# Ten projection tiles as five pairs of two by two block products, seven products for eight, joined on VectorE

## The chip, the cores and the metric

The kernel runs on one core of a Trainium2 chip. The time is device microseconds (us) of one execution. Before the change three executions took 1659.24, 1662.63 and 1664.48 us, median 1662.63. TensorE (PE) multiplies and writes PSUM, VectorE (DVE) does elementwise work, ScalarE (ACT) does activations and copies, GpSimd (POOL) does elementwise work on SBUF only and starts some of the DMAs, SyncE (SP) starts the others.

## The reference

One decoder layer with four parallel token mixers, then a mixture of experts, for 1024 prompt tokens and 8 sample tokens (1032 in all). Everything is float32. The part that matters here is the first projection and what the RWKV mixer does with its first seven tiles:

```python
proj = h @ lw['w_in']                     # h: 1032 x 1024; first 21 tiles of 128 columns feed the mixers
prev = jnp.concatenate([shift0[:, None, :], p[:, :-1]], axis=1)
q = p + (prev - p) * lw['rwkv_mu']        # "interpolation" with the token before, on 7 of the tiles
```

The other tiles feed a pooling branch (2 tiles), a convolution branch (4) and a state-space branch (8). 32 more tiles of the same projection are gates. What is computed stays the same in the changed kernel up to rounding, since a seven-product scheme adds and subtracts blocks before and after the products.

## The kernel before

The normalised input lies in SBUF as `H`, 128 partitions by 8 slices (`k`) by 1032 tokens. A projection tile is a 1024 by 128 piece of the weights (512 KB), stored as eight 128 by 128 blocks in one of the two halves of the ring `wring`. For each tile PE runs three chunks of 344 tokens. A chunk is eight matmuls, one for each `k`, accumulated in one PSUM bank (`half`, L499). A float32 matmul appears in the trace as two weight loads and two matmul records, so a chunk is 16 records and a tile 48.

Tiles 0 to 2 have code of their own (L514, L520, L534), since the norm is still being computed. Tiles 3 to 12 are `pairs(1, 3)` and `pairs(3, 6)`. Tile 13 is cut into pieces that stand between the small products of the RWKV branch (L551, L562). Then come `pairs(7, 10)`, the first gate tiles, and a loop of eight steps in which gate tiles fill PE between small dependent products. The last sections are the branch outputs (L812), the output projection (L861) and the experts (L961, L975).

ACT copies each finished chunk from PSUM into its slot of `PR` (`evac`, L1029) and counts the semaphore `evac`. PE waits for `evac` before it writes a bank again. SP loads the next tile into the ring half that has come free, after a count of `dense` (finished chunks).

In the stretch of tiles 3 to 12 DVE does one thing: when seven RWKV tiles are in SBUF (`evac` 21) it interpolates them, three instructions for each (L1373 to L1375). When two pooling tiles are there (`evac` 27), POOL runs the windowed sums of the pooling branch (L1900 to L1927), about fifty instructions in a row.

The order on each engine is written out by hand. Nothing is scheduled.

Of the kernel before, what the change touches and what calls it, by code (L numbers as in the profile page):

```python
# [57 lines left out]
ROUND = 1.5 * 2 ** 23  # L58
GUESS = [0, 4, 8, 13]
# [80 lines left out]
def build(nc, ins, outs):  # L140
    ctx = ExitStack()
    with ctx:
# [88 lines left out]

        x_t = carve(0, KT, T)
# [42 lines left out]

        block = ctx.enter_context(nc.Block())
# [29 lines left out]
        def mm_of(t, k):  # L306
            return 7 * t + k + (2 if t or k > 1 else 0)

        def ev_of(t, k):
            return 2 + 11 * t + k  # L310

        def sum_of(t, k):
            return k if t == 0 else 4 * t + 4 + k
# [46 lines left out]
        def _(sp):  # L360
# [15 lines left out]
            for j in range(1, N_BR0 // 2 + 1):  # L376
# [106 lines left out]
        def _(pe):  # L483
# [53 lines left out]
            pairs(1, 3)  # L537
            pairs(3, 6)


# [5 lines left out]
            for t in range(2):  # L546
                pe.wait_ge(sem("lora_act"), t + 3)
                if t == 1:
                    pe.wait_ge(sem("k_ss"), 1)
                for c in range(NCH):  # L550
                    mm = pe.matmul(ps[:, 3 + c, 0:CW], bones, TM[:, t, chunk(c)], start=True, stop=True)  # L551
                mm.then_inc(sem("head_sum"), 1)
                tile13(1, 2 * t, 2 * t + 2)
# [263 lines left out]
            def turn(p):  # L817
                m, b = rows_of(ORD[p]), 4 + 2 * (p % 2)
                pe.wait_ge(sem("h2_row"), p + 1)
                if p == 0:  # L820
                    pe.wait_ge(sem("out_c"), 2)
# [46 lines left out]
            for t in range(4):  # L868
# [5 lines left out]
                if t == 0:  # L874
                    for h in range(2):
                        pe.wait_ge(sem("out_c"), h + 1)
# [6 lines left out]
                pe.wait_ge(sem("out_ev"), ev_of(t - 1, 11) if t else 1)  # L883
                pe.wait_ge(sem("op_sum"), sum_of(t, 3))
                if t == 0:
                    pe.wait_ge(sem("op_sum"), 4 + 2)
# [3 lines left out]
                pe.wait_ge(sem("out_c"), 2 + t + 1)  # L890
# [9 lines left out]
                if t == 0:  # L900
                    pe.wait_ge(sem("op_sum"), 4 + 3)
# [3 lines left out]
                if t == 0:  # L905
                    pe.wait_ge(sem("op_sum"), 4 + 4)
# [99 lines left out]
        def _(act):  # L1006
# [37 lines left out]
            for t in range(2):  # L1044
                A(TM[:, t, :], row(S_K + t), ACT.Square, scale=v("kkw", t)).then_inc(sem("lora_act"), 1)
# [192 lines left out]
            def norm_row(p):  # L1238

                n, m = ORD[p], rows_of(ORD[p])  # L1240
                act.wait_ge(sem("out_ev"), ev_of((p - 1) // 2, 7 if p % 2 else 11) if p else 2)
# [77 lines left out]
        def _(dve):  # L1319
# [44 lines left out]


            dve.wait_ge(sem("evac"), 21)
            dve.wait_ge(sem("pads"), 1)
            dve.wait_ge(sem("h_ready"), KT + 1)
            nc.vector.tensor_copy(shift_out[:, :, :], PR[:, S_R:S_R + 7, PAD + TP - 1:]).then_inc(sem("lerp"), 1)
            dve.wait_ge(sem("lerp"), 1)  # L1370
            for t in range(7):
                s = S_R + t
                tt(TM[:, t % 2, 0:TP], PR[:, s, PAD - 1:PAD + TP - 1], row(s, 0, TP), SUB)  # L1373
                link(tt(TM[:, t % 2, TP:T], shift_in[:, t, :], row(s, TP, T), SUB))
                stt(row(s), TM[:, t % 2, :], v("mu", t), row(s), MUL, ADD).then_inc(sem("lerp"), 1)  # L1375
# [315 lines left out]
            def weight_sum(j, left, right):  # L1691

                if j:
                    dve.wait_ge(sem("op_sum"), 4 + j)
# [9 lines left out]
            for h in range(2):  # L1704
                r_ = X2[0:NSMP, NTT - 1, h * HALF:(h + 1) * HALF]
                dve.wait_ge(sem("out_mm"), h + 2)
# [10 lines left out]
            for t in range(4):  # L1717
                bank = [ps[:, (7 * t + k) % 3, :] for k in range(7)]
                (r11, r12), (r21, r22) = ([X2[:, 2 * t + s, h * HALF:(h + 1) * HALF] for h in range(2)] for s in range(2))
                dve.wait_ge(sem("out_c"), 2 + t + 1)  # L1720
# [487 lines left out]
```

## Time and profile before

| | |
|---|---|
| median of three executions | 1662.63 us |
| profiled execution, its own time | 1668.07 us |
| span of the profiled execution | 1666.3 us |
| PE busy | 1549.1 us (93%) |
| DVE busy | 690.7 us (41%) |
| ACT busy | 351.8 us (21%) |
| POOL busy | 200.8 us (12%) |
| mean granted TensorE clock | 0.970 of 2.4 GHz |

PE is the engine to look at. Over 84% of the span the chain that ended last runs through it. Line L499, which holds the projection tiles and gate tiles, has 37% of the span alone. Busy times count what the engine does, not whether the end waits for it. Idle time of DVE, ACT or POOL costs nothing unless PE stands and waits for them.

### The profile page before, as it was taken

What the parts mean: (1) busy time and instruction counts of PE and PEld (TensorE: products, weight loads), DVE (VectorE), ACT (ScalarE), POOL (GpSimd) and SP (SyncE); (2) the same over time, 40 slices, a digit from 0 to 9 for tenths busy, and PEclk for the clock granted to TensorE, in tenths of its full rate; (3) what the DMA queues carried; (4) which work ended last, traced back from release to release, by engine and by line L of the source; (5) the groups of instructions that cost most, each with busy time, mean ns of one, the idle gap of its engine ahead of it and who ended that gap; (6) DMA issues with size and microseconds to landing.
All of it is one profiled execution on the core that took longest, in us unless ns stands there. A gap on an engine that the chain in (4) does not pass through costs nothing.

```text
span 1666.3 us, 20478 instructions
## 1 busy us (share of the span) xinstructions
PE 1549.1 (93%) x7925; PEld 971.2 (58%) x7925; DVE 690.7 (41%) x1300; ACT 351.8 (21%) x653; POOL 200.8 (12%) x316
## 2 busy tenths in 40 slices
PE   8999999999999999999999999999999298888965
PEld 5666666577777777777777865666444232222312
DVE  5130069943343535436353433577844401101106
ACT  3000230231313131313313135000122111111113
POOL 3006300012111111111010010100000001101100
PEclk9999999999999999999999999999999599989987
DMA  6111111021421322121113121474200958766547
GB/s 197 38 39 39 35 37 39 27 111 53 114 64 53 115 52 63 44 72 47 44 39 122 52 92 42 152 289 174 112 38 30 370 196 334 260 226 236 204 153 294
DMA packets 47377, 195.73 MB, mean 117 GB/s; under 512 B 6424, under 2 KB 6920, under 8 KB 42416
## 3 DMA queue, kind: packets, MB, share of 16 engines
q1 hardware_dynamic: 28288, 117.18, 20.3%
q0 software_dynamic: 18992, 77.25, 12.9%
q8 instruction: 63, 1.03, 0.3%
q14 instruction: 34, 0.28, 0.1%
HBM read 357.43 MB, written 41.44 MB: 239 GB/s over the span
## 4 chain that ended last, share of the span: by engine, by line
PE 84%; DMA 5%; DVE 4%; issue 2%; SPq 2%; ACT 2%; POOL 0%; DVEq 0%; POOLq 0%; ACTq 0%
PE ps L499 37%; PE ps L812 7%; PE ps L961 6%; PE ps L861 6%; PE ps L975 4%; PE ps L756 3%; DMA arena<-in_w_gu 3%; PE ps L670 2%; PE ps L665 2%; PE ps L675 2%; PE ps L648 2%; SPq L428 1%; PE ps L514 1%; PE ps L940 1%; PE ps L520 1%
## 5 line engine op out<-in xcount | busy, mean ns | idle before, releaser
L499 PE MATMUL ps<-arena,wring 128*128 128x344 f32 x2208 | 667.2, 452 | 0.0
L499 PEld LDWEIGHTS ps<-arena,wring 128*128 128x128 f32 x2208 | 405.1, 189 | 191.0 <-issue 1.9
L961 PE MATMUL ps<-arena,scr 128*32 128x512 f32 x1280 | 151.8, 620 | 20.3 <-DMA arena<-in_w_gu 20.3
L1955 POOL DMA_DIRECT2D gate_scratch<-stage x96 | 52.3, 545 | 619.7 <-ACT stage L1101 544.1
L812 PE MATMUL ps<-arena,wring 128*128 128x344 f32 x384 | 111.2, 451 | 0.0
L961 PEld LDWEIGHTS ps<-arena,scr 128*32 128x32 f32 x1280 | 39.0, 112 | 116.1 <-issue 82.6
L812 PEld LDWEIGHTS ps<-arena,wring 128*128 128x128 f32 x384 | 72.5, 189 | 38.6
L975 PE MATMUL ps<-arena,scr 128*32 128x512 f32 x640 | 79.6, 642 | 13.7 <-issue 12.3
L1101 ACT ACTIVATE stage<-ps 128x344 f32<-128x344 f32 x84 | 38.4, 458 | 253.6 <-PE ps L499 253.5
L1843 DVE TENSOR_TENSOR scr<-scr,ps 128x256 f32<-128x256 f32 x20 | 8.4, 421 | 187.1 <-ACT scr L1284 187.1
L1540 DVE TENSOR_TENSOR scr<-scr,ps 128x512 f32<-128x512 f32 x40 | 27.5, 688 | 127.8 <-PE ps L670 127.8
L1414 DVE SCALAR_TENSOR_TENSOR arena<-arena,vec 128x1024 f32<-128x1024 f32 x60 | 74.4, 1283 | 1.1
L1029 ACT ACTIVATE arena<-ps 128x344 f32<-128x344 f32 x57 | 25.9, 458 | 225.1 <-PE ps L499 208.0
L975 PEld LDWEIGHTS ps<-arena,scr 128*32 128x32 f32 x640 | 22.9, 118 | 69.6 <-issue 68.0
L756 PE MATMUL ps<-arena,wring 128*128 128x344 f32 x192 | 59.1, 469 | 3.3 <-ACT stage L1075 3.3
L861 PE MATMUL ps<-arena,scr 128*128 128x512 f32 x128 | 58.2, 599 | 0.0
L756 PEld LDWEIGHTS ps<-arena,wring 128*128 128x128 f32 x192 | 37.6, 197 | 24.5 <-ACT stage L1075 3.9
L1141 ACT ACTIVATE scr<-ps 128x512 f32<-128x512 f32 x40 | 23.9, 597 | 130.4 <-PE ps L665 130.4
L2072 POOL DMA_INDIRECT y_rows<-scr,idx x20 | 19.6, 982 | 246.4 <-DVE scr L1856 241.7
L665 PEld LDWEIGHTS ps<-scr 128*128 128x128 f32 x320 | 41.9, 191 | 8.0
L670 PEld LDWEIGHTS ps<-scr 128*128 128x128 f32 x320 | 41.9, 191 | 8.0
L1856 DVE COPY scr<-ps 128x512 f32<-128x512 f32 x20 | 13.8, 692 | 74.0 <-PE ps L975 74.0
(430 smaller groups left out, 1883.7 us busy)
## 6 DMA issues: line engine op xcount, KB each, us to landing
arena<-in_w_gu SPq DMA_DIRECT2D x336, 512.0 KB
arena<-in_w_dn SPq DMA_DIRECT2D x84, 1024.0 KB
wring<-in_w_all SPq DMA_DIRECT2D x61, 512.0 KB, 3.6
gate_scratch<-stage POOLq DMA_DIRECT2D x96, 172.0 KB, 2.2
arena<-gate_scratch POOLq DMA_DIRECT2D x4, 2064.0 KB, 9.5
scr<-gate_scratch POOLq DMA_DIRECT2D x4, 2064.0 KB, 9.5
arena<-y_rows SPq DMA_DIRECT2D x16, 512.0 KB, 10.8
arena<-in_w_out SPq DMA_DIRECT2D x2, 2048.0 KB, 14.9
```

Of the source, the lines that this page charges most:

```text
L499: mm = pe.matmul(ps[:, c, 0:CW], wring[:, slot, k, :], H[:, k, chunk(c)], start=k == 0, stop=k == KT - 1)
L648: mm = pe.matmul(ps[:, 4 + n, (q % 2) * 256:(q % 2) * 256 + 256], (BT if n < 2 else KTB)[:, q, :], KR[:, q, :, :].rearrange("p a b -> p (a ...
L665: mm = pe.matmul(ps[:, 6, q * P:(q + 1) * P], NLB[:, q, :], U[:, q, :], start=True, stop=True)
L670: mm = pe.matmul(ps[:, 7, q * P:(q + 1) * P], TT[:, q, :], X1[:, q, :], start=True, stop=True)
L756: mm = pe.matmul(ps[:, 6 + m % 2, 0:CW], wring[:, n % 2, k, :], H[:, k, chunk(c)], start=k == 0, stop=k == KT - 1)
L812: mm = pe.matmul(ps[:, m % 6, 0:CW], wring[:, n % 2, 2 * b + k, :], row(2 * b + k, c * CW, (c + 1) * CW), start=k == 0, stop=k == 1)
L861: mm = pe.matmul(ps[:, bank, :], left[:, k, :], right[:, k, :], start=k == 0, stop=k == 3)
L961: mm = pe.matmul(ps[S * j:S * (j + 1), i % 2, :], XT[i % 2][:, k * P + S * j:k * P + S * (j + 1)], GU[j][:, k * 2 * HID:(k + 1) * 2 * HID] ...
L975: mm = pe.matmul(ps[S * j:S * (j + 1), 5 + h, :], ATB[:, k, S * j:S * (j + 1)], DN[j][:, k * D + h * HALF:k * D + (h + 1) * HALF], start=k ...
L1101: A(stage[:, c, :], ps[:, c, 0:CW], ACT.Sigmoid).then_inc(sem("evac"), 1)
L1414: ins_ = ts(dst, src, w, v("conv_b", t), MUL, ADD) if j == 0 else stt(dst, src, w, dst, MUL, ADD)
L1955: pool.dma_start(gate_scratch[:, g:g + 1, chunk(c)], stage[:, c:c + 1, :]).then_inc(sem(f"gate_out{c}"), 16)
```

## The change

PE now makes tiles 3 to 12 in five pairs (`pair_tiles`, L620 of the changed kernel). A pair is a product of 1024 by 256 weights with 1024 by 1032 tokens. It is cut into two halves along all three sides: 512 rows, 128 columns (one tile), 516 tokens. Seven block products take the place of eight. Each is done in two quarters of 258 tokens, four matmuls each. The seven results rotate through six PSUM banks.

DVE makes the sums and differences of the weight blocks (`pair_sums`, four for each pair), once those of the tokens (`weight_sum_in`, four in all), and it joins the products (`pair_add`, 14 for each pair). ACT only copies the first product of each pair to SBUF. The seven interpolations (`lerp`) no longer stand in a row. They stand between the joins of the pairs 2 and 3. The weights of a pair lie in two places at once, so a second pair of buffers is used in turn with the ring. The interpolation and two ScalarE squares use other scratch (`TML` in place of `TM`).

```diff
+        PAIRW = [[kk_ring(0), kk_ring(1)], [wring[:, 1, :, :], wring[:, 0, :, :]]]
+        BS = [carve(4 * HT2 * j, 4, HT2) for j in range(4)]          # HT2 = 516, QT = 258
...
 SP:
+            load_pair(0, (0,))
+            sp.wait_ge(sem("dense"), 3)
+            load(2, 0)
+            load_pair(0, (1,))
+            sp.wait_ge(sem("dense"), 9)
+            load_pair(1)
+            for t in range(2, NPAIR):
+                sp.wait_ge(sem("dense"), 6 * t + 3)
+                load_pair(t)
...
 PE:
-            pairs(1, 3)
-            pairs(3, 6)
+            def pair_tiles(t):
+                wa, wb = PAIRW[t % 2]
+                left = (wa[:, 0:4, :], wa[:, 4:8, :], AS[1], AS[0], AS[3], AS[2], wb[:, 4:8, :])
+                right = ((H[:, 0:4, :], 0), (H[:, 4:8, :], 0), (BS[1], None), (BS[0], None), (H[:, 4:8, :], 1), (BS[2], None), (BS[3], None))
+                sums = (0, 0, 3, 1, 4, 2, 0)
+                weight_sums = (0, 0, 2, 1, 0, 3, 4)
+                last_read = (None, 1, 3, 5, 7, 10, 13)
...
+                for k in range(7):
+                    for q in range(2):
+                        g = 14 * t + 2 * k + q
+                        if g < 6:
+                            pe.wait_ge(sem("evac"), min(9, 7 + g))
+                        else:
+                            t0, k0, q0 = (g - 6) // 14, (g - 6) % 14 // 2, g % 2
...
+                        if sums[k] and q == 0:
+                            pe.wait_ge(sem("op_sum"), psum(t, sums[k]))
...
+                        for j in range(4):
+                            mm = pe.matmul(ps[:, g % 6, 0:QT], left[k][:, j, :], src[:, j, c], start=j == 0, stop=j == 3)
...
 ACT:
-            for j in range(1, 3):
-                evac(2 * j + S_R + 1, 6 * j + 3)
-                evac(2 * j + S_R + 2, 6 * j + 6)
-            for j in range(3, 6):
-                evac(2 * j - 6, 6 * j + 3)
-                evac(2 * j - 5, 6 * j + 6)
+            for t in range(NPAIR):
+                for q in range(2):
+                    act.wait_ge(sem("out_mm"), pmm(t, 0, q))
...
+                    A(PQ[q], ps[:, (14 * t + q) % 6, 0:QT], ACT.Copy).then_inc(sem("out_c"), 1)
...
 DVE:
+            def pair_sums(t):
...
+                tt(AS[0], wb[:, 0:4, :], wb[:, 4:8, :], ADD).then_inc(sem("op_sum"), 1)
+                tt(AS[2], wa[:, 0:4, :], wb[:, 0:4, :], SUB).then_inc(sem("op_sum"), 1)
...
+            def pair_add(t, k, dst, left, q, after=None):
...
+                ins_ = tt(dst, left, ps[:, (14 * t + 2 * k + q) % 6, 0:QT], ADD)
+                if q and k in (4, 6):
+                    ins_.then_inc(sem("evac"), 3)
...
+                for q in range(2):
+                    pair_add(t, 5, row(nb)[:, cols(1, q)], VQ[q], q)
+                    pair_add(t, 5, row(nb)[:, cols(0, q)], UQ[q], q)
+                if t < NPAIR - 1:
+                    pair_sums(t + 1)
+                for q in range(2):
+                    pair_add(t, 6, row(nb)[:, cols(0, q)], row(nb)[:, cols(0, q)], q, pev(t, 10 + 2 * q))
...
+            pair_sums(0)
+            weight_sum_in(0, H[:, 0:4, HT2:T], H[:, 0:4, 0:HT2])
...
+            pair_joins(0)
+            pair_joins(1)
...
+            pair_joins(2, (0, 1, 2, 3))
+            pair_joins(3, (4, 5, 6))
+            pair_joins(4)
```

On PE, at the start of tile 3, this stood before. Two chunks are shown; `w_in1` is the load of the tile, `evac` the copy out of the bank.

```order
L499 MATMUL ps<-arena,wring 128x344 [waits w_in1,evac]
L499 MATMUL ps<-arena,wring 128x344 x7
L499 MATMUL ps<-arena,wring 128x344 [waits evac]
L499 MATMUL ps<-arena,wring 128x344 x7
L499 MATMUL ps<-arena,wring 128x344 [waits evac]
```

In the changed kernel PE has this where pair 4 starts. The end of pair 3 stands first, then the products 0, 1 and 2 of pair 4. `out_ev` and `evac` are counts of DVE's joins, and `op_sum` counts its block sums.

```order
L620 MATMUL ps<-scr,wring 128x258 [waits out_ev]
L620 MATMUL ps<-scr,wring 128x258 x3
L620 MATMUL ps<-arena 128x258 [waits out_ev,w_in0,w_in1]
L620 MATMUL ps<-arena 128x258 x3
L620 MATMUL ps<-arena 128x258 [waits evac]
L620 MATMUL ps<-arena 128x258 x3
L620 MATMUL ps<-arena 128x258 [waits out_ev]
L620 MATMUL ps<-arena 128x258 x3
L620 MATMUL ps<-scr,arena 128x258 [waits op_sum,out_ev]
```

A chunk of eight matmuls of 344 tokens has become one of four matmuls of 258, and the waits are now for DVE where they were for ACT.

On DVE the seven interpolations stood in a row before, with nothing around them that PE waits for. The start of that row:

```order
L1369 COPY shift_out<-arena 128x63 [waits h_ready,pads,evac]
L1373 TENSOR_TENSOR scr<-arena 128x1024 [waits lerp]
L1374 TENSOR_TENSOR scr<-shift_in,arena 128x8
L1375 SCALAR_TENSOR_TENSOR arena<-scr,vec,arena 128x1032 [waits dve_self]
L1373 TENSOR_TENSOR scr<-arena 128x1024
```

In the changed kernel this is what DVE does in pair 3, from the last of its three interpolations on. L1475 is a join, L1484 to L1486 an interpolation, L1460 to L1465 the sums for pair 4.

```order
L1475 TENSOR_TENSOR arena<-arena,ps 128x258 [waits out_ev,out_mm] x2
L1484 TENSOR_TENSOR arena<-arena 128x1024
L1485 TENSOR_TENSOR arena<-shift_in,arena 128x8
L1486 SCALAR_TENSOR_TENSOR arena<-arena,vec 128x1032 [waits dve_self]
L1475 TENSOR_TENSOR arena<-arena,ps 128x258 [waits out_ev,out_mm] x2
L1475 TENSOR_TENSOR arena<-arena,ps 128x258 [waits out_mm] x4
L1460 TENSOR_TENSOR arena<-arena 128x512 [waits w_in0,w_in1,out_mm]
L1461 TENSOR_TENSOR arena<-arena 128x512
L1463 TENSOR_TENSOR arena<-arena 128x512 [waits op_sum]
L1465 TENSOR_TENSOR arena<-arena 128x512 [waits op_sum]
L1475 TENSOR_TENSOR arena<-arena,ps 128x258 [waits out_ev,out_mm]
L1475 TENSOR_TENSOR arena<-arena,ps 128x258 [waits out_ev,dense]
```

The interpolations moved in among joins whose results free PE's banks, and the sums for pair 4 stand behind all of them.

## Rows read from the trace of the kernel before

**Rows 1.** Busy time of PE, PEld, DVE, ACT, POOL by stretch; then clock, DMA share, GB/s.

```profile
53.20:192.10 138.90, 138.90 (x482) 90.65 (x481) 17.85 (x22) 13.75 (x31) 44.18 (x62) 1.00 0.14 40
192.10:215.80 23.70, 22.69 (x73) 12.48 (x71) 2.46 (x2) 11.20 (x11) 0.00 (x0) 1.00 0.08 22
```

**Rows 2.** Chain of waits from 50 us on: start us, us, what.

```profile
53.23 138.83 PE ps L499 x480
```

**Rows 3.** Chain of waits in the stretch of the branch outputs.

```profile
1062.75 111.05 PE ps L812 x384
```

**Rows 4.** Timeline of PE around one 256-token group: start us, us, engine, line.

```profile
439.05 3.62 PE L648 MATMUL ps<-scr 128*128 128x256 f32 x16
442.51 3.92 PE L499 MATMUL ps<-arena,wring 128*128 128x344 f32 x13
```

**Rows 5.** Timeline of the weight loads of a 128-token group.

```profile
363.57 1.15 PEld L665 LDWEIGHTS ps<-scr 128*128 128x128 f32 x8
```

**Rows 6.** Groups of DVE by form: count | busy us, mean ns | idle before.

```profile
L1684 DVE TENSOR_TENSOR scr<-arena 128x512 f32<-128x512 f32 x4 | 2.8, 689 | 0.0
L1695 DVE TENSOR_TENSOR arena<-arena 128x2048 f32<-128x2048 f32 x4 | 9.1, 2285 | 0.1
L1843 DVE TENSOR_TENSOR scr<-scr,ps 128x256 f32<-128x256 f32 x20 | 8.4, 421 | 187.1 <-ACT scr L1284 187.1
L1373 DVE TENSOR_TENSOR scr<-arena 128x1024 f32<-128x1024 f32 x7 | 8.5, 1218 | 0.0
L1375 DVE SCALAR_TENSOR_TENSOR arena<-scr,vec,arena 128x1032 f32<-128x1032 f32 x7 | 9.1, 1294 | 0.2
```

**Rows 7.** Groups of POOL by form, the three costliest of the pooling sums.

```profile
L1918 POOL TENSOR_SCALAR scr<-scr,cst 64x1008 f32<-64x1008 f32 x4 | 11.2, 2806 | 0.4
L1920 POOL TENSOR_TENSOR arena<-scr,arena 64x1024 f32<-64x1024 f32 x4 | 8.7, 2171 | 0.3
L1906 POOL TENSOR_TENSOR scr<-arena 128x1040 f32<-128x1040 f32 x2 | 3.8, 1921 | 0.2
```

**Rows 8.** Timeline of POOL and DVE where both work on SBUF.

```profile
462.81 2.96 POOL L1964 COPY scr<-arena 64x256 f32<-64x256 f32 x6
463.26 0.69 DVE L1543 TENSOR_TENSOR scr<-scr,ps 128x512 f32<-128x512 f32 x1
463.86 0.77 DVE L1544 TENSOR_TENSOR scr<-scr,cst 128x512 f32<-128x512 f32 x1
```

**Rows 9.** Single lines, ns min/median/max: 374 to 382 us (first two), whole span.

```profile
L1964 POOL COPY scr<-arena x6: 396/399/762, 375.9 to 378.5; 64x256 f32<-64x256 f32 x6
L1550 DVE SCALAR_TENSOR_TENSOR scr<-arena,vec,scr x6: 339/410/517, 377.6 to 379.5; 128x128 f32<-128x128 f32 x6
L1544 DVE TENSOR_TENSOR scr<-scr,cst x32: 682/685/776, 369.7 to 939.0; 128x512 f32<-128x512 f32 x32
```

**Rows 10.** Chain of waits where PE waits for a DVE result.

```profile
199.11 0.03 issue
199.14 0.02 DVEq L1379
199.16 0.05 issue
199.21 1.24 DVE scr L1380
200.45 0.14 issue
```

**Rows 11.** Group of the first small product behind the projection tiles.

```profile
L551 PE MATMUL ps<-scr,cst 128*128 128x344 f32 x12 | 4.0, 467 | 0.7 <-ACT scr L1045 0.4 <-DVE scr L1380 0.3
```

**Rows 12.** Timeline of DVE, before tile 3 and behind its convolution chain.

```profile
47.04 0.16 DVE L1363 TENSOR_SCALAR smallv<-vec 128x2 f32<-128x2 f32 x1
...
323.65 1.23 DVE L1428 TENSOR_TENSOR arena<-ps,arena 128x1032 f32<-128x1032 f32 x1 [0.18 <-PE ps L597]
```

**Rows 13.** Loads of projection tiles, from issue to landing.

```profile
DMA to landing us min/median/max: 3.4/3.6/15.6
```

More of the change, by code:

```diff
@@ L58 @@
 ROUND = 1.5 * 2 ** 23
+NPAIR = 5
+HT2 = T // 2
+QT = T // 4
 GUESS = [0, 4, 8, 13]
@@ L274, in build, with cols, pmm, pev @@
         V1, V2, V3, V4, V5 = (carve(2 * j * T, 2, T) for j in range(5))
+        PAIRW = [[kk_ring(0), kk_ring(1)], [wring[:, 1, :, :], wring[:, 0, :, :]]]
+        BS = [carve(4 * HT2 * j, 4, HT2) for j in range(4)]
+        AS = [arena[:, HO + KT * T + 2 * TP + 512 * j:HO + KT * T + 2 * TP + 512 * (j + 1)].rearrange("p (k m) -> p k m", k=4)
+              for j in range(4)]
+        PQ = [row(11, QT * q, QT * q + QT) for q in range(2)]
+        UQ = [row(10, QT * q, QT * q + QT) for q in range(2)]
+        VQ = [row(10, QT * q + 2 * QT, QT * q + 3 * QT) for q in range(2)]
+        TML = PR[:, 12:14, PAD:]
+        def cols(side, q):
+            return slice(side * HT2 + q * QT, side * HT2 + (q + 1) * QT)
+        def pmm(t, k, q):
+            return 13 * t + 2 * k + q + 1
+        def pev(t, i):
+            return 12 * t + i - (1 if i > 8 else 0)
+        def psum(t, i):
+            return i if t == 0 else 4 + 4 * t + i
         block = ctx.enter_context(nc.Block())
@@ L375, in _, with load_pair @@
             load(1, 1)
-            for j in range(1, N_BR0 // 2 + 1):
+            def load_pair(t, tiles=(0, 1)):
+                for s in tiles:
+                    n = 3 + 2 * t + s
+                    sp.wait_ge(sem(f"w_in{n % 2}"), 16 * (n // 2))
+                    sp.dma_start(PAIRW[t % 2][s].rearrange("p k m -> p (k m)").unsqueeze(1), ins["w_all"][:, bass.ds(n, 1), :]
+                                 ).then_inc(sem(f"w_in{n % 2}"), 16)
+            load_pair(0, (0,))
[7 more added lines that the diff above has]
+                load_pair(t)
+            sp.wait_ge(sem("dense"), 33)
+            sp.wait_ge(sem("w_in1"), 16 * 6)
+            load(13, 1)
+            sp.wait_ge(sem("w_in0"), 16 * 7)
+            load(14, 0)
+            sp.wait_ge(sem("dense"), 42)
+            load(15, 1)
+            for j in range(8, N_BR0 // 2 + 1):
                 sp.wait_ge(sem("dense"), 6 * j - 3)
@@ L1044, in _ @@
             for t in range(2):
-                A(TM[:, t, :], row(S_K + t), ACT.Square, scale=v("kkw", t)).then_inc(sem("lora_act"), 1)
+                A(TML[:, t, :], row(S_K + t), ACT.Square, scale=v("kkw", t)).then_inc(sem("lora_act"), 1)
             for t in range(2):
@@ new lines, in pair_add @@
+            def pair_add(t, k, dst, left, q, after=None):
+                if (k, q) == (6, 1):
+                    dve.wait_ge(sem("dense"), 6 * t + 15)
+                else:
+                    dve.wait_ge(sem("out_mm"), pmm(t, k, q))
+                if after:
+                    dve.wait_ge(sem("out_ev"), after)
+                ins_ = tt(dst, left, ps[:, (14 * t + 2 * k + q) % 6, 0:QT], ADD)
+                if q and k in (4, 6):
+                    ins_.then_inc(sem("evac"), 3)
+                else:
+                    ins_.then_inc(sem("out_ev"), 1)
```

101 lines of the change are left out of this document (80 added, 21 removed).

## Prediction

> **What bounds the kernel now.** I read four views in this order. First the busy times by stretch: from 53.2 to 192.1 us, where tiles 3 to 12 are made, PE is busy for 138.90 of 138.90 us at the full granted clock, while DVE has 17.85 us of work and ACT 13.75 [rows 1]. The stretch is PE's alone. Second the chain of waits: it runs through these tiles as one piece of 138.83 us with 480 records and no gap [rows 2]. So each us that PE saves here is a us off the end, as long as nothing else becomes late. Third the groups of DVE and POOL by form, for the prices of what is added [rows 6, 7]. Fourth the timeline where DVE and POOL work on SBUF together, since the change puts DVE work beside POOL's pooling sums [rows 8, 9].
>
> **PE's part.** A record of 344 tokens costs 138.83 / 480 = 289.2 ns. At two cycles for a token, 344 tokens are 286.7 ns at 2.4 GHz, which leaves 2.5 ns fixed. A record of 258 tokens then costs 215.0 + 2.5 = 217.5 ns. The nearest group of the trace has 256 tokens: from its start to the start of the next group 3.46 us pass for 16 records, or 216.3 ns [rows 4], so 218 ns for 258. The changed kernel has 5 pairs x 7 products x 2 quarters x 4 matmuls = 280 matmuls, 560 records. That is 121.8 us at 217.5 ns and 122.1 at 218. I take **17.0 us saved**; the ends are 16.7 and, had the fixed part been nothing, 18.4.
>
> Do shorter records expose the weight loads? A load takes 0.19 us, and 0.217 is still more. Loads can also follow faster than their own length: eight of them end within 1.15 us where the matmuls have 128 tokens, so (1.15 - 0.19) / 7 = 0.137 us apart [rows 5]. I count nothing. Do more waits cost? In the branch outputs every four records stand behind a wait, and 384 records take 111.05 us, again 289.2 ns each [rows 3]. A wait that is already met costs PE nothing.
>
> **Loads.** SP issues the same ten tiles, now in pairs, one pair ahead. A load lands 3.6 us after its issue, at worst 15.6 [rows 13]; a pair of tiles has the 24.4 us of the pair in front. Two loads one after the other, since each waits for the one before in its half, are 7 us. Nothing.
>
> **DVE's and ACT's part without POOL.** Queued operations start about 0.09 us before the one in front seems to end (463.26 to 463.86 for a 0.69 us operation [rows 8]), so I take a join of 258 tokens from PSUM at 0.34 us (421 ns for 256 [rows 6]), a weight sum of 512 at 0.60, an interpolation (1218 + about 160 + 1294 ns) at 2.55 and a token sum of 2064 at 2.2 [rows 6]. Pair 0: DVE is free at 47.2 us [rows 12], four weight sums and four token sums are 11.2 us, done by 58.5. PE starts the pair at 53.2, needs token sum 1 (the second) at 60.2 and the last at 74. Hidden. A product (two quarters) takes PE 3.48 us. Two joins and one interpolation are 3.23, so DVE keeps up, barely. At the end of a pair: four joins (1.4), four weight sums (2.4), two joins (0.7), and PE asks for the third sum and the first of these joins two products into the next pair. In pair 3, which starts at 53.2 + 3 x 24.36 = 126.3, DVE is through with these by 150.8, and PE asks at 157.7. That is 6.9 us to spare, and between 133.7 and 150.8 DVE has 14.0 us of work in 17.1, so 3 us of idle time can also be eaten. **DVE may lose 10 us in pair 3 before PE stands.**
>
> ACT copies ten quarters where it copied thirty chunks, less than before.
>
> **The end of the stretch.** Tile 13 used to find its bank free. Its first chunk now waits for `evac` 37, which comes only with the very last join of pair 4. From PE to DVE 0.10 us, the join 0.42, from DVE back to PE 0.14 [rows 10, 6]: **0.7 us lost**. Against this, ACT finishes its squares long before PE wants them, since the interpolations end in pair 3 and ACT is free after the two copies at the start of pair 4. The idle time of 0.4 us in front of the first small product [rows 11] goes: **0.4 gained**. Behind it everything starts from the end of tile 13. The long convolution chain on DVE, which is done only 0.2 us ahead of PE at 323.65 [rows 12], starts from it too, so both shift together. The gate tiles, the output products and the experts' weight loads are all triggered by PE's progress. I see nothing tied to absolute time.
>
> **POOL's part, the cost I can bound only.** POOL's pooling sums start at `evac` 27. That was the copy of tile 8, 53.2 + 6 x 13.9 + 0.5 = 137 us; now it is the last join of pair 2, at 127.4. POOL has 44.2 us of work [rows 1], much of it in operations of 1.9 to 2.8 us that stand back to back (ten of them average (11.2 + 8.7 + 3.8) / 10 = 2.37 us [rows 7]). Before, DVE was idle then. Now pair 3 has three interpolations and four weight sums in this stretch, 13 DVE operations with both inputs in SBUF. The trace shows what such neighbours do. Beside six POOL copies of 0.40 us, a DVE operation with one input in PSUM keeps its 0.69 us (L1543), while the one with both in SBUF goes from 685 ns to 0.77 us (L1544), and of six small ones, 339 ns at the least, the median is 410 and the longest 517 ns; one copy goes from 399 to 762 ns, about until the DVE operation ended [rows 8, 9]. So they take turns, and a DVE operation waits for some part of POOL's: 0.17 of 0.40 us in the small ones.
>
> The page "SBUF — State Buffer" of the Trainium skill (Who interferes with whom) says the same against this change: a VectorE instruction with two SBUF inputs contends with a GpSimd instruction that reads SBUF, and one that has the port keeps it for the whole instruction. The trace agrees in who is slowed: L1544 is and L1543 is not. By that rule each of the 13 could wait for a whole POOL operation.
>
> Let w be the mean wait of the 13. PE's stall is 13 w - 10, and not below 0. Bounds: w = 0 gives no stall; a whole large operation, 2.3 us, gives 20 us. The same part as in the small ones, 0.17 / 0.40 of 2.37, is w = 1.0 and 3 us; half an operation, as for one that arrives at any time, is 1.15 and 5 us. The joins have a PSUM input and do not wait. I take the first, **3 us lost**, near the start of pair 4. Pair 4 has no interpolation and no sums, so it ends there. The granted clock is 1.00 in both stretches of [rows 1], the second with 1.0 us of standing in it; that a stall of 3 us would lower it is not in the sum.
>
> **The sum.** -17.0 + 0.7 - 0.4 + 3.0 = -13.7 us. Against the profiled execution's own time, 1668.07 us, that is 1654.4. This execution lies 5.4 us above the median of the three, so for the median: 1662.63 - 13.7 = **1648.9 us**. Executions of before lie 5.2 us apart, so about 0.3% either way is what a measurement cannot tell from no change.
>
> **Rivals.**
>
> *DVE never makes PE stand.* POOL gives way, or its waits stay under 10 us. For it: the slack is large. Against it: the 0.77 us and the 517 ns. Gain 17.0 - 0.3 = 16.7, time 1645.9.
>
> *DVE and POOL alternate operation for operation.* Each of the 13 waits for a whole large POOL operation. For it: half and more of the six small DVE operations were slowed. Against it: POOL also has dozens of 0.2 us operations, the first of a row waits half an operation only, and the 8-token parts of the interpolations hide in the gaps. Stall 13 x 2.3 - 10 = 20, net 17.0 - 0.3 - 20 = -3.3, time 1666; with the 2.8 us operations (26.4) 1672. It costs more than the products save from w = 2.05 on. This is the case on the slow side.
>
> *The pitch does not follow the tokens.* If 258-token records with a new weight block each took 250 ns instead of 217.5 (operands changing between two regions, sums just written), 560 records would be 140 us and the gain gone: 1663. For it: nothing of 258 tokens is in the trace. Against it: the 216.3 ns beside 256 tokens.
>
> *Half is given back later.* The shift lets some transfer or DVE chain behind 320 us become the last to arrive. 1655. For it: DVE's 0.2 us of slack at 323.65. Against it: its chain starts at the same trigger as PE's.
>
> **How the numbers follow.** The forecast (stall of 1 to 7 us) 0.54; no stall 0.22; alternation in full 0.08; pitch 0.05; half given back 0.11. "Faster by over 0.3%" (5 us) takes the first, the second and nearly all of the last: 0.86. "Within 0.3%": part of the pitch and of the alternation, and a bit of the last: 0.09. "Slower": 0.05. The range goes from the no-stall case less a us and a half of spread, 1644, to 1658, which takes in the given-back case and a stall of up to 12 us.
>
> **What would show it.** 560 records on L620 at 217 to 218 ns of pitch; PE's idle time in front of L620 near the product 2 of pair 4, put down to DVE's sums, of about 3 us and nothing at pairs 1 to 3; L1484 and L1486 at 1.22 and 1.29 us in pair 2, and longer in pair 3; the last weight sum for pair 4 at about 160 us; tile 13 starting 0.3 us behind the last product, and all that follows earlier by one amount, up to the end. The prediction is wrong if PE stands at each pair, if the pitch is above 225 ns, or if the shift at the start of the output products is not the one at tile 13.

## The result and the profile after

| | before | after |
|---|---|---|
| median of the executions | 1662.1 us (1659.24 to 1664.48) | 1644.06 us (1640.15 to 1647.82) |
| profiled execution, its own time | 1668.07 us | 1640.67 us |
| PE busy | 1549.1 us | 1523.1 us |
| DVE busy | 690.7 us | 741.2 us |
| mean granted TensorE clock | 0.970 | 0.974 |

After to before is 0.9894, 95% interval 0.9874 to 0.9915: faster by 17.6 us (14.1 to 20.9). Forecast were 13.7 us and 1648.9, from 1644 to 1658. The time lies inside by 0.06 us, at the fast edge. Of the runs below, three executions (4185, 4186 and 1865 us) were disturbed and are left out of every median and range.

The chain of waits (start us, us, what) around the pairs:

```profile
52.35 121.81 PE ps L620 x560
174.16 0.03 DVEq L1474
174.20 0.04 issue
174.24 0.43 DVE arena L1475
174.68 0.04 issue
174.72 4.90 PE ps L552 x16
179.62 1.75 PE ps L639 x6
```

560 records follow each other at 121.81 / 560 = 217.5 ns with no gap. In this place stood 138.83 us [rows 2]. Then comes the stop ahead of tile 13, from 174.16 to 174.72. The first small product (L639) starts straight behind the first chunk of tile 13.

Busy time of PE, PEld, DVE, ACT, POOL by stretch, with clock, DMA share and GB/s, which answers to [rows 1]:

```profile
52.35:174.16 121.81, 121.80 (x560) 105.91 (x559) 62.71 (x110) 9.81 (x16) 44.12 (x48) 1.00 0.13 44
174.16:191.30 17.14, 15.99 (x52) 9.37 (x52) 2.89 (x3) 3.14 (x3) 5.24 (x15) 1.00 0.10 11
```

DVE's work in the stretch has gone from 17.85 to 62.71 us, half of the stretch, and PE never waits for it. The joins, as a group, and the two large parts of the interpolations, as single lines (ns min/median/max):

```profile
L1475 DVE TENSOR_TENSOR arena<-arena,ps 128x258 f32<-128x258 f32 x70 | 27.8, 420 | 58.6 <-PE ps L620 58.2
```

```profile
L1484 DVE TENSOR_TENSOR arena<-arena x7: 1210/1219/1376, 108.5 to 141.5; 128x1024 f32<-128x1024 f32 x7
L1486 DVE SCALAR_TENSOR_TENSOR arena<-arena,vec x7: 1292/1294/3458, 109.8 to 142.9; 128x1032 f32<-128x1032 f32 x7
```

DVE stood idle for 58.2 us ahead of joins because PE had not finished. The reverse did not happen. Of the 14 large parts of interpolations one was held up for long, 3458 ns. The timeline of DVE and POOL shows by what:

```profile
130.83 2.81 POOL L2084 TENSOR_SCALAR scr<-scr,cst 64x1008 f32<-64x1008 f32 x1
132.50 0.42 DVE L1475 TENSOR_TENSOR arena<-arena,ps 128x258 f32<-128x258 f32 x1 [1.32 <-PE ps L620]
132.84 1.22 DVE L1484 TENSOR_TENSOR arena<-arena 128x1024 f32<-128x1024 f32 x1
...
134.18 3.46 DVE L1486 SCALAR_TENSOR_TENSOR arena<-arena,vec 128x1032 f32<-128x1032 f32 x1
134.20 2.35 POOL L2086 TENSOR_TENSOR arena<-scr,arena 64x1024 f32<-64x1024 f32 x1
...
148.35 0.69 DVE L1463 TENSOR_TENSOR arena<-arena 128x512 f32<-128x512 f32 x1
149.08 0.69 DVE L1465 TENSOR_TENSOR arena<-arena 128x512 f32<-128x512 f32 x1
...
149.91 1.92 POOL L2072 TENSOR_TENSOR scr<-arena 128x1040 f32<-128x1040 f32 x1
```

L1486 ended 1.09 us behind POOL's TENSOR_TENSOR, so it had waited for nearly all of it. L1484 beside POOL's TENSOR_SCALAR kept its 1.22 us. The weight sums fell among POOL's operations of 8 tokens and kept 0.69. So the 13 operations in pair 3 waited 3458 - 1294 + 1376 - 1219 ns and little else, 2.3 us: w was 0.18 us, not 1.0. The last weight sum for pair 4 ended at 149.8 us, where the prediction had about 160. POOL's next row of four large TENSOR_TENSORs began at 149.91, 0.14 us behind it.

How the shift travels is read from the chain of waits, us from one mark to the next. The marks are the start of tile 3, the first of the branch gates (L756 before, L844 after), the start of the output products, and the first reload of `y_rows`. The last column is the granted clock of the 272 to 282 us ahead of that reload.

| execution | to branch gates | to output | to y_rows | clock |
|---|---|---|---|---|
| before, three executions | 933.39, 933.31, 933.18 | 197.43, 194.71, 194.72 | 440.1, 436.0, 438.9 | 0.94, 0.95, 0.94 |
| after, three executions | 916.38, 916.63, 916.29 | 194.72, 197.54, 194.71 | 434.3, 432.3, 435.0 | 0.96, 0.97, 0.96 |

Up to the branch gates the change gives 933.29 - 916.43 = 16.9 us, and executions agree within 0.3. The middle has two values in both kernels, 2.8 us apart. They come from one group of 16 records behind a stop of 3.34 us, in which PE waits for ScalarE's copies to `stage`. L844 x16 takes 4.89 us in the profiled execution of after and 7.73 in `e_again`, the same program. The granted clock was 1.00 behind the stop in the first and 0.50 in the second. So the same stop may cost 2.8 us of clock or nothing, and the two kernels have to be compared at the same middle value. (`e_adds`, below, lies between the two.) The rest of the medians' gain lies in the last column but one.

### The profile page after: what moved, and what is told of

Its sections match the earlier page's. It is cut to its first block, busy times and chain, and to the rows that moved or that the text cites. A ratio compares the mean times of both kernels' runs of the same rounds, so it can differ in the third digit from the quotient of the medians.

```text
span 1638.9 us, 20757 instructions
## 1 busy us (share of the span) xinstructions
PE 1523.1 (93%) x8005; PEld 985.3 (60%) x8005; DVE 741.2 (45%) x1394; ACT 342.1 (21%) x633; POOL 205.7 (13%) x316
## 4 chain that ended last, share of the span: by engine, by line
PE 84%; DMA 6%; DVE 4%; issue 2%; SPq 2%; ACT 2%; POOL 0%; DVEq 0%; POOLq 0%; ACTq 0%
PE ps L552 29%; PE ps L620 7%; PE ps L900 7%; PE ps L949 6%; PE ps L1049 5%; PE ps L1063 4%; PE ps L844 3%; DMA arena<-in_w_gu 3%; PE ps L758 2%; PE ps L753 2%; PE ps L763 2%; PE ps L736 2%; SPq L481 1%; DMA scr<-h_rows,idx 1%; PE ps L567 1%
## 5 line engine op out<-in xcount | busy, mean ns | idle before, releaser
L552 PE MATMUL ps<-arena,wring 128*128 128x344 f32 x1728 | 528.5, 452 | 0.6 <-DVE arena L1475 0.6
L552 PEld LDWEIGHTS ps<-arena,wring 128*128 128x128 f32 x1728 | 314.4, 189 | 143.5 <-issue 1.9
L1049 PE MATMUL ps<-arena,scr 128*32 128x512 f32 x1280 | 146.7, 605 | 17.0 <-DMA arena<-in_w_gu 17.0
L900 PE MATMUL ps<-arena,wring 128*128 128x344 f32 x384 | 111.2, 451 | 0.0
L900 PEld LDWEIGHTS ps<-arena,wring 128*128 128x128 f32 x384 | 72.5, 189 | 38.6
L1063 PE MATMUL ps<-arena,scr 128*32 128x512 f32 x640 | 78.2, 632 | 16.1 <-issue 14.8
L620 PE MATMUL ps<-scr,arena 128*128 128x258 f32 x288 | 64.3, 381 | 0.0
L844 PE MATMUL ps<-arena,wring 128*128 128x344 f32 x192 | 56.4, 453 | 3.3 <-ACT stage L1163 3.3
L620 PEld LDWEIGHTS ps<-scr,arena 128*128 128x128 f32 x288 | 54.6, 190 | 8.0
L949 PE MATMUL ps<-arena,scr 128*128 128x512 f32 x128 | 58.2, 598 | 0.0
L1475 DVE TENSOR_TENSOR arena<-arena,ps 128x258 f32<-128x258 f32 x70 | 27.8, 420 | 58.6 <-PE ps L620 58.2
L844 PEld LDWEIGHTS ps<-arena,wring 128*128 128x128 f32 x192 | 36.1, 189 | 23.3 <-ACT stage L1163 3.9
```

Of the source, the lines that this page charges most:

```text
L552: mm = pe.matmul(ps[:, c, 0:CW], wring[:, slot, k, :], H[:, k, chunk(c)], start=k == 0, stop=k == KT - 1)
L620: mm = pe.matmul(ps[:, g % 6, 0:QT], left[k][:, j, :], src[:, j, c], start=j == 0, stop=j == 3)
L844: mm = pe.matmul(ps[:, 6 + m % 2, 0:CW], wring[:, n % 2, k, :], H[:, k, chunk(c)], start=k == 0, stop=k == KT - 1)
L900: mm = pe.matmul(ps[:, m % 6, 0:CW], wring[:, n % 2, 2 * b + k, :], row(2 * b + k, c * CW, (c + 1) * CW), start=k == 0, stop=k == 1)
L949: mm = pe.matmul(ps[:, bank, :], left[:, k, :], right[:, k, :], start=k == 0, stop=k == 3)
L1049: mm = pe.matmul(ps[S * j:S * (j + 1), i % 2, :], XT[i % 2][:, k * P + S * j:k * P + S * (j + 1)], GU[j][:, k * 2 * HID:(k + 1) * 2 * HID] ...
```

## The experiments

**The change alone, again.** Unchanged kernels, for the spread: `e_again` and `e_third` are the changed one, `b_again` and `b_third` the one before.

> The changed kernel itself once more, timed in five rounds. Theory: the gain is the 17.0 us of the records (560 at 217.5 ns for 480 at 289.2), less 0.66 us in front of tile 13, plus 0.4 us at the first small product, and nothing else. So the stretch from the first record of tile 3 to the first record after tile 13's first chunk is 16.7 us shorter, and the median of five rounds lies 16 to 18 us below before. Rival: something behind 320 us gained too (the profiled execution was 27 us shorter than the one of before). Then the median is 19 us or more below before, and the start of the output products is again 20 us earlier relative to tile 3, not 17.

Measured: 1641.55 us (1640.71 to 1642.79), before 1664.13, ratio 0.9866 (0.9847 to 0.9885). That is 22.3 us, beyond the 16 to 18 expected. The rival's second sign, 20 us at the start of the output products, did not come: compared at the same middle value it is 16.7 us.

> The kernel before, a second profiled execution. In the first one the part from the first expert product to the last reload of results took 280 us (1344.24 to 1624.19), in the changed kernel 271 to 273 us, though nothing of it was edited. Theory: this part varies by several us from one execution to the next, with the order in which weight loads land; the changed kernel gives 16.6 us up to the output products and nothing there. Then this execution has an expert part somewhere between 271 and 281 us, and 1184.0 us at the start of the output products as before, within 1 us. Rival: the shift makes the expert part itself shorter; then it takes 279 to 281 us again.

Measured: 1659.59 us (one execution), the marks as in the table. The output products start at 1180.4 us and not within 1 us of 1184.0, since the middle took its lower value. The part up to `y_rows` is 4.2 us shorter than in the first execution of the same kernel.

> The kernel before, a third profiled execution. The first two took 933.39 and 933.31 us from tile 3 to the first branch product (L756), 197.4 and 194.7 from there to the output products, and 440.1 and 436.0 from these to the reload of the results. Theory: the first number is fixed (933.3 within 0.2 us), the second takes one of two values about 2.8 us apart (one group of 16 records at the lower clock or not), the third lies anywhere from 432 to 442. Rival (the kernel before is always slower in the experts): the third is 436 or more again.

Measured: 1661.84 us (one execution). The first two numbers came as expected, and the third is 438.9, which fits the theory and the rival.

> The changed kernel, third series. Its first two gave 18.0 and 22.6 us less than before. Theory: up to the first branch product it is 16.9 us earlier (916.4 to 916.6 us from tile 3), and the rest is scatter of the expert part, so over all series the gain draws near to 17, and this one gives 15 to 21 us. Rival (3 to 5 us more are gained in the experts each time): 20 to 23 us.

Measured: 1643.38 us (1641.86 to 1643.51), before 1662.62, ratio 0.9878 (0.9857 to 0.9899). Three comparisons give 17.6, 22.3 and 20.3 us. Their intervals overlap (the last is 16.8 to 23.8), and all three lie above the 16.9 us gained up to the branch gates, the first mark. Only the second interval (19.1 to 25.5) leaves 16.9 out. Both repeated medians lie below 1644, outside the range that was forecast.

**e_pool_late: pooling sums behind the pairs.**

```diff
-            pool.wait_ge(sem("evac"), 27)
+            pool.wait_ge(sem("evac"), 39)
```

> POOL's pooling sums wait for the last join of pair 4 in place of pair 2. Theory: what slowed DVE in pair 3 were POOL's tensor operations. All seven interpolations then take 1.22 and 1.29 us (L1486 at most 1.3 us, where one took 3.46), DVE is through with pair 3's sums 2.3 us earlier relative to PE, and PE's 560 records still take 121.8 us, since the waits were hidden. Rival: the long one is a wait of another kind (PSUM, a semaphore) and stays.

Measured: 1649.63 us (one execution). The long interpolation is gone (all at 1.22 and 1.29 us) and PE has the same 121.81 us for 560 records. So POOL did lengthen it, and it cost PE nothing. But 5.1 us are lost behind tile 13: POOL's sums now run beside the DVE work ahead of the convolution chain, on the path of the small products.

```profile
204.34 1.99 POOL L2086 TENSOR_TENSOR arena<-scr,arena 64x1024 f32<-64x1024 f32 x1
205.17 2.24 DVE L1549 SCALAR_TENSOR_TENSOR arena<-arena,vec,scr 128x1024 f32<-128x1024 f32 x1 [19.57 <-ACT scr L1148]
...
207.47 1.27 DVE L1549 SCALAR_TENSOR_TENSOR arena<-arena,vec,scr 128x1024 f32<-128x1024 f32 x1
```

The first L1549 waits for a TENSOR_TENSOR of POOL's that was there first, and takes 2.24 us where the second takes 1.27. Further waits of this kind follow (L1559 takes 2.02 for 1.29, two L1569 4.35 for 2.38), and at the first product behind this chain (L1594) DVE is 3.4 us late. Where the other 1.7 us go was not followed. The place of the pooling sums is a good one.

**e_row: the interpolations in a row again, ahead of pair 2's joins.**

```diff
-            pair_joins(2, (0, 1, 2, 3))
-            pair_joins(3, (4, 5, 6))
+            for t in range(7):
+                lerp(t)
+            pair_joins(2)
+            pair_joins(3)
```

> All seven interpolations stand in a row in front of pair 2's joins, none between the joins. Theory: seven at 2.55 us are 17.8 us, from the last join of pair 1 (about 101.5 us in the changed kernel) to 119.5; PE asks for the first join of pair 2 at its product 4, at 115.0. It stands 4 to 6 us there and nowhere else; 1648 to 1650 us. Rival (the placing is of no use, six banks are enough): stall under 1 us, time as the changed kernel's.

Measured: 1653.12 us (1647.76 to 1655.04), ratio 0.9927 (0.9901 to 0.9952). PE stands 5.27 us for a join, and for some us behind it has not its full clock:

```profile
120.38 5.23 PE L620 MATMUL ps<-arena 128*128 128x258 f32 x16 [5.27 <-DVE arena L1475]
```

```profile
120.38:122.50 2.12, 2.12 (x5) 1.75 (x6) 1.61 (x5) 0.00 (x0) 0.00 (x0) 0.50 0.00 0
122.50:125.50 3.00, 3.00 (x13) 2.54 (x13) 0.42 (x1) 0.00 (x0) 0.00 (x0) 0.85 0.02 5
```

The clock column reads 0.50 behind the stop, the lower level of 1.2 GHz. The 272 records from the stop to the end of the pairs take 60.92 us, 1.8 more than at 217.5 ns each, so the 5.27 us stop costs 7.0. Up to the branch gates this kernel takes 923.36 us, 6.9 more than the changed one. So spreading the interpolations is what keeps PE fed. The stall is in the expected 4 to 6 us, the time is 3 to 5 us above the expected one, and the part up to `y_rows` was long here (441.4 us, table below). In pair 3 the weight sums now meet POOL's large operations:

```profile
155.76 2.24 POOL L2079 TENSOR_TENSOR scr<-scr 128x1034 f32<-128x1034 f32 x1
156.15 2.39 DVE L1461 TENSOR_TENSOR arena<-arena 128x512 f32<-128x512 f32 x1
158.07 2.69 POOL L2080 TENSOR_TENSOR scr<-scr 64x1026 f32<-64x1026 f32 x1
158.58 2.73 DVE L1463 TENSOR_TENSOR arena<-arena 128x512 f32<-128x512 f32 x1
160.86 3.12 POOL L2086 TENSOR_SCALAR scr<-scr,cst 64x1008 f32<-64x1008 f32 x1
161.34 1.47 DVE L1465 TENSOR_TENSOR arena<-arena 128x512 f32<-128x512 f32 x1
```

2.07 (L1460), 2.39, 2.73 and 1.47 us instead of 0.69. The first three waited for a TENSOR_TENSOR to its end, the last for 0.8 us at the start of a TENSOR_SCALAR, 5.9 us in all. PE did not stand for them, since they stayed within DVE's slack.

**e_adds and e_adds_pool_late: eight adds of two SBUF inputs in front of pair 4's joins**, where the large pooling operations are, and the same with the pooling sums behind the pairs.

```diff
+            for j in range(8):
+                ins_ = tt(row(6 + j % 4), H[:, 0, :], H[:, 1, :], ADD)
...
             pair_joins(4)
```

> Eight additions of 1032 elements with both inputs in SBUF are added on DVE between the joins of pair 3 and of pair 4, where POOL runs four long TENSOR_TENSOR operations in a row (1.9 to 2.4 us), then a TENSOR_SCALAR of 2.8 us. Their result is not used. Theory (turns, a TENSOR_TENSOR of POOL keeps the port to its end): four of the additions take 1.2 + up to 1.9 us, the ones beside the TENSOR_SCALAR 1.2 to 1.4; together 9.3 + 6 to 8 = 15 to 17 us from 150.4 us, done at 166 to 168, while PE asks for the first join of pair 4 at 163.7: stall of 2 to 5 us, time 1647. Rival (POOL always gives way, DVE's one long operation was chance): 9.3 us, no stall.

> The eight additions as before, but POOL's pooling sums wait for the last join of pair 4, so that POOL is idle beside them. Theory (POOL's tensor operations blocked the additions): they take 8 x 1.16 = 9.3 us in place of 18.9, PE's records take 121.8 us without a stop, in place of 130. The late pooling sums then meet DVE behind tile 13, where DVE's chain leads to the end, and cost about 5 us there, so the time is near 1649 us, as with the late sums alone. Rival (the additions themselves made PE wait): the stall of 6 us stays.

Measured: 1650.24 us (1649.76 to 1650.96), ratio 0.9921 (0.9901 to 0.994), and 1648.88 us (1646.23 to 1652.8), ratio 0.9925 (0.9903 to 0.9946). The eight adds beside POOL's sums:

```profile
150.21 18.92 DVE L1542 TENSOR_TENSOR arena<-arena 128x1032 f32<-128x1032 f32 x8
151.77 2.78 POOL L2080 TENSOR_TENSOR scr<-scr 128x1038 f32<-128x1038 f32 x1
...
157.50 3.23 POOL L2082 TENSOR_TENSOR scr<-scr 64x1026 f32<-64x1026 f32 x1
160.82 3.66 POOL L2088 TENSOR_SCALAR scr<-scr,cst 64x1008 f32<-64x1008 f32 x1
...
169.64 5.84 PE L620 MATMUL ps<-arena 128*128 128x258 f32 x16 [6.08 <-DVE arena L1475]
```

and without them:

```profile
151.50 9.36 DVE L1542 TENSOR_TENSOR arena<-arena 128x1032 f32<-128x1032 f32 x8
```

9.6 us of pure waiting in eight operations. The five adds beside a TENSOR_TENSOR took 2.57, 2.95, 2.94, 3.39 and 3.02 us, and the three beside the TENSOR_SCALAR 2.02, 1.22 and 1.24. Alone each is 1.23. So full alternation with TENSOR_TENSORs, which the prediction had as its slow rival, is real here. The waits and the stall are over what was expected: 18.9 us for 15 to 17, a stall of 6.08 us for 2 to 5, 1650.2 us for 1647. In the changed kernel it did not come about because only one large operation of DVE's meets a TENSOR_TENSOR there. PE stands 6.08 us and then again runs at half clock. The joins, with an input in PSUM, keep their 0.42 us. With the pooling sums late the adds and the time (1648.9 us for 1649) came as expected, so POOL made the adds long.

**e_lump: DVE's slack measured.** Twelve memsets, 13.1 us from the first to the end of the last, ahead of pair 4's weight sums.

```diff
+                if t == 3:
+                    for j in range(12):
+                        ins_ = nc.vector.memset(row(6 + j % 4), 0.0)
...
```

> Twelve memsets of 1032 elements, about 10.7 us of DVE work that reads nothing, stand in pair 3 between the joins of product 5 and the weight sums for pair 4. In the changed kernel the third sum is done 6.7 us before PE asks for it and the first join behind the sums about as long before. Theory: the stall of PE at product 2 of pair 4 is what goes over that, 3.5 to 5 us, plus 1 to 2 us for the clock that falls in it, and nothing elsewhere; 1648 us. Rival (the slack is larger, since six banks and the queue hide more): no stall; or the slack is smaller and PE stands for 9 us.

Measured: 1656.85 us (1653.12 to 1659.25), ratio 0.9963 (0.9947 to 0.9978).

```profile
147.86 0.92 DVE L1516 MEMSET arena<- 128x1032 f32 x1 [0.16 <-issue]
...
160.96 2.08 DVE L1460 TENSOR_TENSOR arena<-arena 128x512 f32<-128x512 f32 x1
...
165.48 8.82 PE L620 MATMUL ps<-scr,arena 128*128 128x258 f32 x32 [8.14 <-DVE arena L1475]
```

The stall is over the expected 3.5 to 5 us, because a memset takes 0.92 us and the next starts 1.09 us after it, 13.1 us in all for the expected 10.7, and one sum takes 1.4 us more. From the last joins of product 5 to the first join behind the sums 18.1 us pass (146.94 to 165.01), and 3.35 in the changed kernel (146.34 to 149.69). So DVE is 14.7 us late and PE stands 8.14: the slack was 6.6 us, where the prediction had 6.9 ahead of PE's request. The time is 9 us above the expected 1648: the first mark comes 10.4 us later than in the changed kernel, where 4.5 to 7 were expected, and the part up to `y_rows` was the longest of all variants (441.8 us). The memsets took 0.92 us beside POOL's small operations and beside its TENSOR_TENSORs alike.

**e_tile13: tile 13's wait one join earlier.** Its bank is free once join 10 of pair 4 has read it. The last join, which takes `evac` from 36 to 39, is asked for ahead of the small products instead.

```diff
+                if c == 0 and lo == 0:
+                    pe.wait_ge(sem("out_ev"), pev(NPAIR - 1, 10))
-                half(1, c, lo, hi, 6 * 6 + 3 + c - 2, 16 * 6 + 16)
+                half(1, c, lo, hi, 6 * 6 + 3 + c - 2 if c else None, 16 * 6 + 16)
...
+                if t == 0:
+                    pe.wait_ge(sem("evac"), 39)
```

> The first chunk of tile 13 waits for the joins that last read its own bank (product 5, first quarter) and not for the last join of pair 4; the wait for that one stands in front of the first small product, 4.6 us later. Theory: the 0.57 us in which PE stands in front of tile 13 goes, and everything behind starts 0.57 us earlier relative to tile 3, since DVE and ACT take their start from tile 13 too. Time 0.6 us below the changed kernel, within its noise. Rival: the DVE chain behind tile 13 takes the end over, and the product group of the output projection starts no earlier.

Measured: 1644.96 us (1642.06 to 1646.91), ratio 0.9897 (0.9878 to 0.9916).

```profile
174.34 4.63 PE ps L552 x16
```

The stop is gone, the 16 records take 4.63 us instead of 4.90, and the first mark comes after 915.74 us, 0.7 less than in the changed kernel. It is the best version by this mark. The medians can't tell it from the change.

**e_repeat10 and e_repeat5: PE's time put back.** Ten (five) of the 70 quarters are made twice, with the same result.

```diff
+                        if k in (1, 4) and q == 1:        # (4,) in e_repeat5
+                            for j in range(4):
+                                pe.matmul(ps[:, g % 6, 0:QT], left[k][:, j, :], src[:, j, c], start=j == 0, stop=j == 3)
```

> The changed kernel with ten of its 70 quarters of products made twice (the four matmuls of a quarter, then the same four again), so that PE is busy for 10 x 8 x 217.5 ns = 17.4 us more in the pairs and everything behind starts within about 0.6 us of where it starts before the change. Nothing stands for it: DVE gets more time. From tile 3 to the first branch product: 916.4 + 17.4 = 933.8 us (before: 933.2 to 933.4). What it tells apart is where the rest of the medians' gain comes from: in three executions each, the part from the output products to the first load of y_rows takes 436.0 to 440.1 us before and 432.3 to 435.0 in the changed kernel, and that goes with the granted clock of its last 275 us (0.94 to 0.95 before, 0.96 to 0.97 after). Theory A: the clock there hangs on when in the execution this part runs. Then with the start put back the part takes 436 to 440 us again at 0.94 to 0.95, and the time is about 1662, level with before. Theory B: it comes from something that the change leaves behind (no such thing is known in that part, whose instructions are the same). Then it stays at 432 to 435 at 0.96 to 0.97, and the time is about 1642.5 + 17.4 = 1660, 3 to 4 us under before. Theory C: three executions each are a chance draw; then any value from 432 to 440.

> The same with five quarters made twice, 5 x 8 x 217.5 ns = 8.7 us more of PE. From tile 3 to the first branch product: 916.4 + 8.7 = 925.1 us. Theory B: the part of the output and the experts takes 432 to 435 us at a clock of 0.96 to 0.97, time about 1651. Theory A: it hangs on the start, so it may lie at either level (of two earlier variants that start at about this place one took 433.9 and one 441.4), and the time is 1651 or about 1656.

Measured: `e_repeat10` 1662.8 us (1655.2 to 1663.92), before 1662.0, ratio 0.9994 (0.9979 to 1.0009); `e_repeat5` 1654.32 us (1649.61 to 1657.82), ratio 0.995 (0.9932 to 0.9968). All variants by their marks:

| execution | to branch gates | to output | to y_rows | clock |
|---|---|---|---|---|
| e_repeat10 | 933.76 | 194.72 | 438.4 | 0.96 |
| e_repeat5 | 925.55 | 197.48 | 436.6 | 0.95 |
| e_row | 923.36 | 194.71 | 441.4 | 0.94 |
| e_lump | 926.83 | 194.71 | 441.8 | 0.94 |
| e_adds | 925.16 | 196.09 | 433.9 | 0.96 |
| e_adds_pool_late | 920.58 | 194.72 | 434.4 | 0.97 |
| e_pool_late | 921.57 | 197.68 | 435.6 | 0.96 |
| e_tile13 | 915.74 | 197.59 | 433.3 | 0.97 |

With 17.4 us of PE put back, nothing of the gain is left: -1.0 us by the ratio, interval -3.5 to +1.5, and +0.8 by the medians. The first mark is 933.76 as expected. So the gain goes with PE's shorter products, and what else the change moved is worth nothing that this interval could tell. Theory B expected 3 to 4 us to remain. The interval reaches only its edge. The part up to `y_rows` is back at 438.4 us, but its clock reads 0.96, not the 0.94 to 0.95 of theory A. With one profiled execution of each variant this isn't settled: the length may move with where the part starts, or be a chance draw (theory C). Of the variants that start between the two kernels, four lie at 434 to 437 us and two above 441, and the two long ones have the lowest clock. Two rows show what the clock goes with:

```profile
1340.00:1618.90 278.90, 239.87 (x2040) 78.66 (x2037) 30.58 (x60) 40.27 (x66) 35.07 (x36) 0.94 0.63 228
```

```profile
1323.60:1598.50 274.90, 236.00 (x2044) 79.11 (x2040) 30.56 (x60) 40.36 (x66) 34.97 (x36) 0.96 0.63 231
```

The first row is the third execution of before, the second that of after: the same work on all engines, PE busy 3.9 us longer at the lower clock, and the stretch 4.0 us longer. What decides which clock is granted there isn't settled.

`e_repeat5` shows one thing more. Its first mark is 925.55 and not 925.1. Here the change stands at another place in time against POOL's sums, and the weight sums for pair 4 meet the row of large TENSOR_TENSORs:

```profile
153.49 2.00 DVE L1463 TENSOR_TENSOR arena<-arena 128x512 f32<-128x512 f32 x1
155.41 2.40 DVE L1464 TENSOR_TENSOR arena<-arena 128x512 f32<-128x512 f32 x1
157.84 2.28 DVE L1466 TENSOR_TENSOR arena<-arena 128x512 f32<-128x512 f32 x1
160.16 2.73 DVE L1468 TENSOR_TENSOR arena<-arena 128x512 f32<-128x512 f32 x1
...
156.09 7.12 PE L623 MATMUL ps<-arena 128*128 128x258 f32 x32
163.27 7.23 PE L623 MATMUL ps<-scr,arena 128*128 128x258 f32 x32
```

The four sums take 9.41 us for 2.76. The interpolations of pair 3 waited 2.3 us besides, so w is 9.0 / 13 = 0.7 us. The 32 records from 156.09 on are 6.96 us of work, and the next ones start after 7.18: PE stands 0.2 us in front of product 2 of pair 4, the place that the prediction named, and loses 0.3 us there in all. In `e_repeat10` the 13 operations waited 10.2 us, w = 0.8, and PE didn't stand (640 records in 139.21 us). There a repeated quarter in front of product 2 of pair 4 gives DVE 1.7 us more.

## Why the prediction was right

- **Products, -17.0 us: right.** 560 records in 121.81 us are 217.5 ns each, the figure worked out from the fixed 2.5 ns. The rival of a worse pitch is dead, and weight loads stay hidden.
- **Loads: right.** No record of the pairs waits for one.
- **Tile 13, +0.7: right.** The stop is 0.57 us (the prediction's list of signs says 0.3), and the 16 records behind it take 4.90 us instead of the 4.63 that they take in e_tile13, where the stop is gone: 0.84 together.
- **ACT's squares, -0.4: right, and a bit small.** The first small product follows tile 13 with no gap. Its six records take 1.75 us, where behind the stop of before they took 2.02: 0.27 more, which the sum has not.
- **The stall from POOL and DVE, +3.0: mis-sized.** It is 0. The step that failed is "The same part as in the small ones, 0.17 / 0.40 of 2.37, is w = 1.0". w was 0.18 us. The mechanism is there, and stronger than taken: a large TENSOR_TENSOR of POOL's holds a DVE operation with two SBUF inputs to its end (3.46 us; eight adds 18.92 instead of 9.36). But the two have to meet. In the changed kernel POOL's first large TENSOR_TENSORs run while DVE waits for PE, and the weight sums fall among POOL's 8-token operations. The average over POOL's work was the wrong measure. The place in time was the right one. That w is so low is luck: the last sum ended 0.14 us before POOL's row of large operations began, and in e_repeat5 and e_repeat10, where they met, w was 0.7 and 0.8. That PE hardly stands is not: with 0.7 and the slack of the changed kernel it stood 0.2 us, near the nothing that the prediction's own 13 w - 10 gives. With 0.8 and 1.7 us more slack it didn't stand. The page "SBUF — State Buffer" of the Trainium skill (Who interferes with whom) says that a two-input VectorE instruction contends with a GpSimd instruction that reads SBUF. The trace agrees for TENSOR_TENSOR (3.46 us for 1.29). For TENSOR_SCALAR it agrees less: L1484 keeps 1.22 us beside one of 2.81, and the longest wait beside one is 0.8 us (e_row, e_adds).
- **The clock in a stall: left out, and not small.** "That a stall of 3 us would lower it is not in the sum." Stops of 5.27, 6.08 and 8.14 us cost 1.8, 2.4 and 1.9 us more (e_row, e_adds, e_lump). 0.27 us of this is what 16 records lose behind a stop of 0.57 us too, at full clock. The stop of 3.34 us in front of L844, near the forecast's 3 us, cost 2.8 us in one execution and nothing in another. For the 20 us stall of the alternation no run shows the price.
- **The shift travels to the end: right, with an addition.** -17.0 + 0.84 - 0.4 - 0.27 = -16.8 against -16.9 measured at the branch gates, where executions lie within 0.3 of each other. No transfer and no chain gave anything back. The sign named for it, the same shift at the start of the output products, holds only at the same middle value: the two profiled executions differ by 19.7 us there, 2.8 of which are the clock behind one stop. The medians gain 1 to 5 us more, in the output and expert part, which the prediction had at zero. No run shows what sets that part's length.

The measured time is nearest to the first rival, no stall (1645.9). The forecast's own case, a stall of 1 to 7 us, did not come about. The direction and the size of the main term hold. That the time lies in the range is luck: the first series is inside by 0.06 us, and the two repeated ones (1641.55 and 1643.38) are below it.

## What to carry over

Work out a new pitch from the fixed part and the part for each token of the nearest records, then count records: that term came out to 0.1%. Contention between two engines isn't an average: lay the two timelines on each other and ask which operation meets which, and whether the slack covers it. Then shift the meeting by a few us in a variant, to see if the answer was luck. When a variant's median moves by more than its first mark does, put the saved time back and see if the rest returns, before a reason is given to it.

## What the runs showed of the hardware

- A large POOL TENSOR_TENSOR (1.9 to 2.4 us) held DVE operations with two SBUF inputs to its end (3.46 us for 1.29; sums 2.07 to 2.73 for 0.69; adds 2.57 to 3.39 for 1.23). A POOL TENSOR_SCALAR held them less: not at all (1.22 us beside one of 2.81), 1.38 for 1.22 at most in the changed kernel, 1.47 for 0.69 in e_row and 2.02 for 1.23 in e_adds. DVE's joins with a PSUM input (0.42 us) and memsets (0.92 us) kept their time.
- POOL pays too: its TENSOR_SCALAR of 2.81 us takes 3.66 and its TENSOR_TENSOR of 1.92 takes 2.78 beside DVE's adds.
- After PE had stood for 5.27 us the granted clock read 0.50 in the next 2.1 us, after 6.08 us in the next 4. After the stop of 0.57 us it stayed at 1.00. After one stop of 3.34 us it was 1.00 in one execution and 0.50 in another of the same program.
